# First gated product of a two-block transformer kernel: ten of its eleven column pairs computed as seven block products, with the sums of the fifth modulation row moved ahead of it

## The chip, the core and the metric

One NeuronCore of one Trainium2 chip runs the whole program in one launch. The metric is the device time of that launch in microseconds, and the figure for a kernel is the median of its runs.

## What is computed

Two transformer blocks run one after the other on 512 tokens of width 1024, all in float32. The part that the change rewrites is the gated product of the first block's feed-forward layer, with 2816 hidden features:

```python
h2 = _rmsnorm(x, norm2_w) * (1.0 + scale2) + shift2
ffn = jnp.dot(jax.nn.silu(jnp.dot(h2, w_ffn_gate)) * jnp.dot(h2, w_ffn_up), w_ffn_down)
x = x + gate2 * ffn
```

`gate2` is one of six rows of a modulation `jnp.dot(silu(c), w_ada) + b_ada`; the kernel calls the rows groups 0 to 5, and `gate2` is group 5.

## The kernel before

**Three-pass products.** Each float32 operand is split in a high part (a ScalarE copy to fp32r, L1369 for weights) and a low part (a VectorE subtraction, L1893 for weights), and each product of two operands is three TensorE matmuls: high by high, high by low, low by high (`mm3`). Activations stand split in `Hh`/`Hl` (8 blocks of 128 features by 512 tokens); weights are split, one chunk of 128 x 1024 at a time, into slots of `wh`/`wl` (4 slots) and, in the stages that allow it, two more in `Ah`/`Al`.

**Chunks and ticks.** `weight_plan()` lists all chunks in the order of their loading; `schedule()` walks over the ticks (a tick is the TensorE work that one visit to one chunk gives) and says at each tick which chunks ScalarE splits (`hi_at`), which VectorE finishes or sums (`done`), and which load is issued (`load_at`). Each engine runs its own program in that order and in strict order: an instruction that waits holds back all behind it on its engine. `w.after(n, f)` puts a piece of work n ticks later in an engine's order. Loads are issued by SyncE into four raw buffers in turn; a load into a buffer waits until the chunk in it before has been split or summed.

**The stages around the change**, in order of time: `rp0`, `rp1` (retention projection), `wo0`, `wo1` (output projection; 16 ticks each, each tick six matmuls of 512 columns), `up` and `dn`. In `rp0` to `wo0` VectorE also sums one modulation row (group 4) from eight `ada4` chunks of `w_ada`, each one `scalar_tensor_tensor` into `ACC` (L1890) that needs only its chunk's landing. In `wo0` it also makes the last of the weight sums of the first down product (the four operations on `CST`). `wo0` and `wo1` end each token tile with a residual, two operations `AR<-bank,G` and `X<-X,AR`.

**The up stage.** Pair 0 (gate and up columns 0 to 255) is computed in two halves of 256 tokens, since the second norm is still finishing: eight ticks of 24 matmuls of 256 columns. Pairs 1 to 10 take four ticks each, one for each chunk of two feature blocks, gate and up columns side by side: 24 matmuls of 512 columns. Then ScalarE takes `silu` of two gate banks (L1672), VectorE multiplies by two up banks (`AR<-AR,bank`), and a subtraction of 256 columns prepares the down product. The eight `ada5` chunks lie among the chunks of pairs 2 and 3, and `row_sum` folds their sum on TensorE ahead of pair 6.

**The down stage** `dn` already works with seven block products, 12 matmuls of 512 columns in a full tick, and takes some of its weights from DRAM sums (`sums_dram`) that were made earlier. The sums for the second block's down product are made by GpSimd-issued DMAs that copy (L2815) and add in DRAM (`second_terms` L2820, `third_terms` L2825, `fourth_term` L2829).

## Time and profile before

| | |
|---|---|
| median of 3 runs | 1527.66 us (1526.28 to 1527.98) |
| profiled execution | 1526.64 us, span 1524.8 us |
| TensorE (PE) | busy 1500.3 us, 98% |
| VectorE (DVE) | busy 999.1 us, 66% |
| ScalarE (ACT) | busy 660.8 us, 43% |
| granted clock of PE | 1.00 of full in the up stage |

Times in rows are microseconds from the start of the span. A matmul's own duration includes its passage through the array, so the pace of a stream is read from the distance of starts. Idle time is given ahead of an instruction, with what ended it; of several releasers the one named can have been done long before, and the true one is then mostly a transfer.

### The profile page before, as it was taken

To read this page: it belongs to the slowest core of one execution; us is meant where nothing else is said; L and a number is where in the kernel's file an instruction comes from. 1 tells how busy PE (TensorE), PEld (TensorE's weight loads), DVE (VectorE), ACT (ScalarE), POOL (GpSimd) and SP (SyncE) were. 2 spreads that over 40 slices of the span, in tenths; PEclk is the share of its full clock that TensorE was granted. 3 is DMA by queue.
4 is the path that set the end of the run, shared out by engine and by line. 5 is a ranking of instruction groups with operands and counts; after the bars stand their busy time and mean duration, and the time that the engine had idled before them with its cause. 6 is when DMAs were issued, how large, how long until landed. Compare 5 with 4: busy or idle time off the path is not lost.

```text
span 1524.8 us, 21037 instructions
## 1 busy us (share of the span) xinstructions
PE 1500.3 (98%) x8527; PEld 1224.8 (80%) x8527; DVE 999.1 (66%) x1729; ACT 660.8 (43%) x1090; POOL 64.4 (4%) x93
## 2 busy tenths in 40 slices
PE   7999999999999999999999989999999999999999
PEld 5777887778888898888887767877788988888887
DVE  6679886776588654323358876787567456556885
ACT  4453334653322442222336553766525434434653
POOL 1000000000000011001000021200011000000000
PEclk9999999999999999999999999999999999999999
DMA  9422122159778498967977516100113222232473
GB/s 386 145 82 97 56 70 83 57 187 352 267 273 308 138 350 287 264 163 185 215 172 216 186 60 221 56 30 29 57 56 125 97 101 87 89 110 97 134 230 126
DMA packets 87018, 237.98 MB, mean 156 GB/s; under 512 B 12037, under 2 KB 12165, under 8 KB 85769
## 3 DMA queue, kind: packets, MB, share of 16 engines
q1 hardware_dynamic: 68312, 204.87, 38.6%
q0 software_dynamic: 18608, 31.77, 9.5%
q8 instruction: 67, 1.10, 0.3%
q14 instruction: 31, 0.25, 0.1%
HBM read 222.94 MB, written 45.35 MB: 176 GB/s over the span
## 4 chain that ended last, share of the span: by engine, by line
PE 90%; DVE 6%; ACT 3%; issue 1%; POOL 0%; DMA 0%; SPq 0%; DVEq 0%; ACTq 0%
PE bank L689 86%; PE bank L701 4%; DVE AR L1915 1%; DVE wl L1893 1%; DVE Hl L1915 0%; ACT wh L1369 0%; DVE G L1922 0%; DVE AR L2225 0%; DVE X L1915 0%; DVE Al L1893 0%; DVE AR L1918 0%; DVE X L1922 0%; ACT AR L1380 0%; DVE ST L1915 0%; DMA CST<-in_cst 0%
## 5 line engine op out<-in xcount | busy, mean ns | idle before, releaser
L1369 ACT ACTIVATE wh<-raw 128x1024 fp32r<-128x1024 f32 (+1 forms) x223 | 230.7, 1036 | 367.7 <-PE bank L689 290.0
L1893 DVE TENSOR_TENSOR wl<-raw,wh 128x1024 fp32r<-128x1024 f32 (+1 forms) x223 | 263.8, 1193 | 102.0 <-ACT wh L1369 101.9
L689 PE MATMUL bank<-wh,Hh 128*128 128x512 f32 (+1 forms) x726 | 293.1, 404 | 3.8 <-DVE wl L1893 2.5
L689 PE MATMUL bank<-wh,Hl 128*128 128x512 f32 (+1 forms) x726 | 281.1, 387 | 0.0
L689 PE MATMUL bank<-wl,Hh 128*128 128x512 f32 (+1 forms) x726 | 280.4, 386 | 0.0
L689 PE MATMUL bank<-Hh,wh 128*128 128x512 f32 (+2 forms) x712 | 268.5, 377 | 0.5 <-DVE Hl L1915 0.4
L689 PE MATMUL bank<-Hl,wh 128*128 128x512 f32 (+2 forms) x712 | 266.9, 375 | 0.0
L689 PE MATMUL bank<-Hh,wl 128*128 128x512 f32 (+2 forms) x712 | 266.9, 375 | 0.0
L689 PEld LDWEIGHTS bank<-wh,Hh 128*128 128x128 f32 x726 | 136.5, 188 | 38.5 <-issue 9.7
L689 PEld LDWEIGHTS bank<-wh,Hl 128*128 128x128 f32 x726 | 136.3, 188 | 28.4
L689 PEld LDWEIGHTS bank<-wl,Hh 128*128 128x128 f32 x726 | 136.8, 188 | 23.6
L689 PEld LDWEIGHTS bank<-Hh,wh 128*128 128x128 f32 (+1 forms) x712 | 133.7, 188 | 25.4 <-issue 0.7
L689 PEld LDWEIGHTS bank<-Hl,wh 128*128 128x128 f32 (+1 forms) x712 | 133.7, 188 | 24.7 <-issue 0.5
L689 PEld LDWEIGHTS bank<-Hh,wl 128*128 128x128 f32 (+1 forms) x712 | 133.7, 188 | 24.6
L1369 ACT ACTIVATE Ah<-raw 128x1024 fp32r<-128x1024 f32 (+1 forms) x58 | 58.3, 1006 | 122.6 <-PE bank L689 89.8
L1922 DVE SCALAR_TENSOR_TENSOR AR<-bank,PRMT,AR 128x511 f32<-128x511 f32 x88 | 63.8, 746 | 51.0 <-ACT AR L1866 49.5
L689 PE MATMUL bank<-Hh,Ah 128*128 128x512 f32 (+1 forms) x256 | 96.3, 376 | 0.0
L689 PE MATMUL bank<-Hl,Ah 128*128 128x512 f32 (+1 forms) x256 | 96.2, 376 | 0.0
L689 PE MATMUL bank<-Hh,Al 128*128 128x512 f32 (+1 forms) x256 | 96.2, 376 | 0.0
L1893 DVE TENSOR_TENSOR Al<-raw,Ah 128x1024 fp32r<-128x1024 f32 (+1 forms) x58 | 65.9, 1156 | 36.6 <-ACT Ah L1369 36.6
L701 PE MATMUL bank<-CST,AR 128*128 128x128 f32 x513 | 79.7, 282 | 10.2 <-DVE AR L1918 9.2
L1915 DVE TENSOR_TENSOR Hl<-AR,Hh 128x512 fp32r<-128x512 f32 (+2 forms) x62 | 55.2, 904 | 47.3 <-ACT Hh L1657 37.2
(275 smaller groups left out, 2014.3 us busy)
## 6 DMA issues: line engine op xcount, KB each, us to landing
raw<-in_wst SPq DMA_DIRECT2D x224, 512.0 KB, 4.5
sums_dram<-in_down POOLq DMA_DIRECT2D x11, 2816.0 KB, 38.0
raw<-sums_dram SPq DMA_DIRECT2D x40, 512.0 KB, 4.1
raw<-in_down SPq DMA_DIRECT2D x30, 512.0 KB, 4.6
CST<-in_down SPq DMA_DIRECT2D x11, 1024.0 KB, 5.9
sums_dram<-CST SPq DMA_DIRECT2D x11, 1024.0 KB, 4.8
AR<-in_wst SPq DMA_DIRECT2D x8, 1024.0 KB, 11.2
X<-in_x SPq DMA_DIRECT2D x8, 512.0 KB, 5.9
```

Of the source, the lines that this page charges most:

```text
L689: return e.matmul(o, l, r, start=start, stop=stop, skip_group_check=True)
L701: return e.transpose(o, a, C("ident")[0:n, 0:n])
L1369: e.activation(HI[slot[i]][:, 0:width(i)], raw[:, i % NR, 0:width(i)], ACT.Copy).then_inc(*w_hi.mark(i))
L1893: e.tensor_tensor(LO[slot[i]][:, 0:n], raw[:, i % NR, 0:n], HI[slot[i]][:, 0:n].bitcast(f32), SUB).then_inc(*w_lo.mark(i))
L1915: return e.tensor_tensor(o, a, b, op).then_inc(*dve.mark(*events))
L1922: return e.scalar_tensor_tensor(out=o, in0=a, scalar=s, in1=b, op0=op0, op1=op1).then_inc(*dve.mark(*events))
```

## The change

Pairs 1 to 10 of the first up product become seven block products (Winograd's form of Strassen's scheme) over two halves of the 1024 features, two halves of the 512 tokens, and gate against up columns. Each product is 512 features by 256 weight columns by 256 tokens: 24 matmuls of 256 columns, one tick. So a pair has seven ticks, where it had four. Four weight blocks are loaded as before (B11, B12, B21, B22; B12 is used in sums alone), and VectorE forms four sums of them in the raw buffers (`up_sum`: T1 = B11+B12, T3 = B12+B22, T2 = B22+T1, T4 = B21+T2); B11, B21, B22 and T1 to T4 are split. Four sums of the activations are formed once (`up_left_sum`) and split into `Ah`/`Al`, `EH`/`EL` and the right halves of `Hh`/`Hl`. `Ah`/`Al` are thus no slots in this stage. Results are combined by three ScalarE copies out of the banks (`snapshot`), two `silu` and five VectorE operations for each pair, beside the subtraction for `dn`.

The raw buffers get fixed homes (`raw_homes`), with two more in `CST` and a third one for one chunk. The `ada5` chunks move ahead: one behind each of the last two chunks of `rp1` (the other chunks there have `ada4`), and so on through `wo0` and `wo1`, and the last, `ada5.7`, behind the last `ada5` of `wo1`'s chunks. `row_sum` of group 5 moves to the seventh tick of pair 0. The third and fourth terms of the DRAM sums move behind the roots of a later stage on GpSimd's queue. The second norm gets four full buffers instead of two.

```diff
@@ -87,14 +87,16 @@
     among = ada((4,), 1)
     for n in (0, 1):
         block(f"rp{n}", "w_ret_proj", 8, [(512 * n, 512)], among=among, start=1 - n)
+    among += ada((5,), 1)
     for n in (0, 1):
         block(f"wo{n}", "w_out", 8, [(512 * n, 512)], among=among)
-    among = ada((5,), 1)
-    for j in range(11):
-        for c in range(4):
-            plan.append((f"up{j}", c, ("w_ffn_gate", "w_ffn_up"), 2 * c, 2, [(256 * j, 256), (256 * j, 256)]))
-            if j > 1 and among:
-                plan.append(among.pop(0))
+    plan += among
+    for c in range(4):
+        plan.append(("up0", c, ("w_ffn_gate", "w_ffn_up"), 2 * c, 2, [(0, 256), (0, 256)]))
+    for j, z in up_splits():
+        at = {"B11": ("w_ffn_gate", 0), "B21": ("w_ffn_gate", 4), "B12": ("w_ffn_up", 0), "B22": ("w_ffn_up", 4)}
+        w, k = at.get(z, (None, 0))
...
@@ -116,6 +118,65 @@
 
 
+def up_steps():
+
+
+    begin = "B11 1,B21 1,B11 2,B21 2,T1 1,T2 1,B22 1,T3 1,T1 2,T4 1,B22 2,T2 2,B11 3,T3 2,T1 3,T4 2,B22 3,T2 3,B21 3,T3 3"
+    steps = [(int(j), z) for z, j in (x.split() for x in begin.split(","))]
+    for j in range(4, 10):
+        steps += [(j, "B11"), (j, "T1"), (j - 1, "T4"), (j, "B22"), (j, "T2"), (j, "B21"), (j, "T3")]
+    return steps + [(10, "T1"), (10, "B11"), (10, "B22"), (10, "T2"), (9, "T4"), (10, "T3"), (10, "B21"), (10, "T4")]
+
+
+def up_splits():
...
+             (2, "B21"): [(2, "T1")], (1, "T4"): [(2, "T3")], (2, "B22"): [(2, "T2")], (2, "T2"): [(2, "T4")],
+             (3, "B11"): [(3, "T1")], (2, "T4"): [(3, "T3")], (3, "B22"): [(3, "T2")], (3, "T2"): [(3, "T4")]}
+    for j in range(4, 11):
+        after.update({(j, "B11"): [(j, "T1")], (j, "T1"): [(j, "T3")], (j, "B22"): [(j, "T2")], (j, "T2" if j < 10 else "B21"): [(j, "T4")]})
+    return after
+
+
+def raw_homes(chunks, place):
+
+
+    home, queue = {}, {}
+    ring, first = place["2ck", 0], place["up0", 0]
...
@@ -257,6 +318,9 @@
 
     def up(prefix):
         ticks.extend((prefix, (0, a, c), place[f"{prefix}0", c], a > 0) for a in (0, 256) for c in range(4))
+        if prefix == "up":
+            ticks.extend((prefix, (j, z), place["up" + z, j], True) for j, z in up_steps())
+            return
         ticks.extend((prefix, (j, 0, c), place[f"{prefix}{j}", c], True) for j in range(1, 11) for c in range(4))
 
     def seven(key):
...
-        if k and name == "up" and ticks[k - 1][0] == "wo1":
-            avail += [(v, place["wo1", 1]) for v in (NH, NH + 1)]
+        if k and name == "dn" and ticks[k - 1][0] == "up":
...
             avail += [(v, place["2wn1", 1]) for v in (NH, NH + 1)]
         here = max(n for n, p in enumerate(plain) if p <= i)
         done[k] += lows
-        used |= set(lows)
+        for x in lows:
+            use(x)
         lows = []
-        while at < ring and at - NR in used:
+        issue(k)
+        while at < ring and (at in loaded or at in made):
+            mine = chunks[at][0][2:3] in ("B", "T") and chunks[at][0][:2] == "up"
...
@@ -592,8 +696,41 @@
         PART = {"1": 0, "5": 0, "7": 1, "6": 1, "2": 2, "3": 2, "4": 3}
         BLOCK = {"dn": "up", "2dn": "2up"}
         SPLIT_AT = {**{2 * n - 7: n for n in range(4, 15)}, 25: 15, 27: 16, 29: 17, 31: 19, 32: 18, 33: 20}
+        SPLITS = {"dn": {0: 2, 2: 3, **SPLIT_AT}, "2dn": SPLIT_AT}
         LEFT_IN = [*range(5)] * 3 + [1, 2, 3, 5, 0, 6]
         SUMS_AT = {2: ("6", 0), 4: ("6", 1), 6: ("6", 2), 8: ("5", 0), 9: ("5", 1), 10: ("5", 2), 12: ("3", 0), 14: ("3", 1), 16: ("3", 2)}
+
+        ACT2 = A(0, 11264).rearrange("p (j m s) -> p j m s", j=11, m=2)
+        PARTS = A(6144, 4096).rearrange("p (t h q) -> p h t q", t=4, h=2)
+        LU, RG = A(11776, 512), A(12288, 512)
...
@@ -1047,9 +1186,13 @@
             by_tile("wo1", ["wo1"], 8, merged, HM, lambda t, n: dve.of(("wo1", t)), lambda t: w.after(TURN[t], lambda: norm_turn("n2", t)))
 
             def up(prefix, tag, freed, fourth=None):
-                for j, a, c in w.steps(prefix):
...
                         if last and c == 3:
                             free[b] = freed(j, m)
+
+            def up_product(j, z):
+                i, b = place["up" + z, j], up_product_bank(j, z)
+                h, l = split_weights(i)
+                xh, xl = UPLEFT[z]
+                first = z in ("B11", "T1", "B21")
+                on.wait_ge(*w_lo.of(i))
+                if z in UPSUM:
+                    on.wait_ge(*dve.of(("up", "left", z)))
+                if first:
+                    claim(b)
+                elif z == "T2":
+                    on.wait_ge(*act.of(("up", "p1", j)))
+                elif z == "T3":
+                    on.wait_ge(*act.of(("up", "u", j)))
+                elif z == "T4":
+                    on.wait_ge(*dve.of(("up", "c22", j)))
+                else:
+                    on.wait_ge(*act.of(("up", "q5", j)))
+                for m in (0, 1):
+                    for q in range(4):
+                        x = mm3(bank[b][:, 256 * m:256 * m + 256], (h[:, q, tok(m)], l[:, q, tok(m)]), (xh[:, q, :], xl[:, q, :]), first and m + q == 0, q == 3)
+                x.then_inc(*dense.mark(("up", z, j), ("used", i)))
+                if z == "T4":
+                    free[b] = act.of(("up", "right gate", j))
+                elif z == "B22":
+                    free[b] = dve.of(("up", "c12", j))
...
@@ -1656,20 +1828,59 @@
                 on.wait_ge(*(freed or left_free(key, n)))
                 e.activation(hi[:, 0:256 * x.shape[1]].rearrange("p (a q) -> p a q", q=256), x, ACT.Copy).then_inc(*act.mark((key, "left", n)))
 
-            for j, a, c in w.steps("up"):
-                if (j, a, c) == (0, 256, 0):
+            def up_left(z, free):
+                on.wait_ge(*dve.of(("up", "sum", z)))
+                on.wait_ge(*free)
+                for u in (0, 1):
+                    e.activation(UPLEFT[z][0][:, :, tok(u)], up_place(z)[:, u, :].rearrange("p (k q) -> p k q", k=4), ACT.Copy).then_inc(*act.mark(("up", "left", z, u)))
+
+            def snapshot(j, z):
+                e.activation(to, bank[up_product_bank(j, z)][:, :], ACT.Copy).then_inc(*act.mark(("up", event, j)))
+
+            def left_silu(j):
+                on.wait_ge(*dve.of(("up", "c11", j)))
+                e.activation(left_gate(j), left_gate(j), ACT.Silu).then_inc(*act.mark(("up", "left gate", j)))
...
-                e.tensor_tensor(LO[slot[i]][:, 0:n], raw[:, i % NR, 0:n], HI[slot[i]][:, 0:n].bitcast(f32), SUB).then_inc(*w_lo.mark(i))
+                e.tensor_tensor(LO[slot[i]][:, 0:n], raw_of(i), HI[slot[i]][:, 0:n].bitcast(f32), SUB).then_inc(*w_lo.mark(i))
+                for t in formed.get(i, ()):
+                    up_sum(t)
+
+            def up_sum(t):
+
+                z, j = chunks[t][0][2:], chunks[t][1]
+                a, b = {"T1": ("B11", "B12"), "T3": ("B12", "B22"), "T2": ("B22", "T1"), "T4": ("B21", "T2")}[z]
+                for q in (a, b):
+                    if q[0] == "B":
+                        on.wait_ge(*landed(place["up" + q, j]))
+                own()
+                tt(raw_of(t), raw_of(place["up" + a, j]), raw_of(place["up" + b, j]), ADD, ("formed", t))
 
             def right_sums(key, p):
                 b11, b12, b21, b22 = (SUMT[:, 512 * q:512 * q + 512] for q in range(4))
```

**VectorE at the end of `wo0` and the start of `wo1`.** Before, from the split of chunk `wo1.1` to the first residual of `wo1` (`bank3` is the residual of `wo0`'s last tile; the `x2` row is the splits of `wo1.2` and `wo1.3`):

```order
L1893 TENSOR_TENSOR wl<-raw,wh 128x1024 [waits s_w_hi]
L1915 TENSOR_TENSOR CST<-CST 128x512 [waits s_pair]
L1915 TENSOR_TENSOR CST<-CST 128x512 [waits s_dve]
L1915 TENSOR_TENSOR CST<-CST 128x512
L1915 TENSOR_TENSOR CST<-CST 128x512 [waits s_dve]
L1915 TENSOR_TENSOR AR<-bank3,G 128x512 [waits s_dense]
L1915 TENSOR_TENSOR X<-X,AR 128x512 [waits s_x3,s_dve]
L1893 TENSOR_TENSOR wl<-raw,wh 128x1024 [waits s_w_hi] x2
L1915 TENSOR_TENSOR AR<-bank0,G 128x512 [waits s_dense]
```

Of the changed kernel, the same stretch:

```order
L2104 TENSOR_TENSOR wl<-raw,wh 128x1024 [waits s_w_hi]
L2138 TENSOR_TENSOR CST<-CST 128x512 [waits s_pair]
L2138 TENSOR_TENSOR CST<-CST 128x512 [waits s_dve]
L2138 TENSOR_TENSOR CST<-CST 128x512
L2138 TENSOR_TENSOR CST<-CST 128x512 [waits s_dve]
L2101 SCALAR_TENSOR_TENSOR ACC<-raw,ST,ACC 128x1024 [waits s_dve,s_raw1]
L2138 TENSOR_TENSOR AR<-bank3,G 128x512 [waits s_dense]
L2138 TENSOR_TENSOR X<-X,AR 128x512 [waits s_x3,s_dve]
L2104 TENSOR_TENSOR wl<-raw,wh 128x1024 [waits s_w_hi]
L2101 SCALAR_TENSOR_TENSOR ACC<-raw,ST,ACC 128x1024 [waits s_dve,s_raw3]
L2101 SCALAR_TENSOR_TENSOR ACC<-raw,ST,ACC 128x1024 [waits s_dve,s_raw0]
L2104 TENSOR_TENSOR wl<-raw,wh 128x1024 [waits s_w_hi]
```

Three sums of `ada5` chunks (5, 6 and 7) now stand here. The last two stand between the split of `wo1.2` and the split of `wo1.3`; `ada5.7` is loaded into buffer 0 (`s_raw0`), which is that of `wo1.2`, and its load waits for the split of `wo1.2`.

**VectorE as the up stage begins.** Of the changed kernel, from the last low part of the second norm to the first half of pair 0's products (before, two weight splits, two products and a subtraction stood here):

```order
L2138 TENSOR_TENSOR Hl<-AR,Hh 128x4x128 [waits s_act] x2
L2138 TENSOR_TENSOR AR<-AR 128x2x512 [waits s_dve] x4
L2138 TENSOR_TENSOR Al<-AR,Ah 128x4x128 [waits s_act] x4
L2104 TENSOR_TENSOR wl<-raw,wh 128x1024 [waits s_w_hi]
L2151 COPY G<-bank6 128x512 [waits s_dve,s_small]
L2151 COPY G<-bank7 128x512
L2104 TENSOR_TENSOR wl<-raw,wh 128x1024 [waits s_w_hi]
L2138 TENSOR_TENSOR raw<-raw 128x1024 [waits s_dve,s_raw3,s_raw1]
L2138 TENSOR_TENSOR AR<-AR,bank2 128x512 [waits s_dense,s_act]
L2138 TENSOR_TENSOR AR<-AR 128x256 [waits s_dve]
L2138 TENSOR_TENSOR AR<-AR,bank3 128x512 [waits s_dense,s_act]
L2104 TENSOR_TENSOR wl<-AR,wh 128x1024 [waits s_w_hi]
```

The `x4` rows are the four sums of the activations and the low parts of two of them; `bank6` and `bank7` are group 5's row.

**VectorE in a pair of the up stage.** Before, for pair 3 (the multiplications with the up banks, and splits):

```order
L1893 TENSOR_TENSOR wl<-raw,wh 128x1024 [waits s_w_hi] x2
L1915 TENSOR_TENSOR AR<-AR,bank2 128x512 [waits s_dense,s_act]
L1915 TENSOR_TENSOR AR<-AR 128x256 [waits s_dve]
L1915 TENSOR_TENSOR AR<-AR,bank3 128x512 [waits s_dense,s_act]
L1893 TENSOR_TENSOR wl<-raw,wh 128x1024 [waits s_w_hi] x2
L1893 TENSOR_TENSOR Al<-raw,Ah 128x1024 [waits s_w_hi] x2
```

Of the changed kernel, most of one pair's round (`CST` and `raw` are raw buffers; rows without `wl` that write them are the weight sums):

```order
L2138 TENSOR_TENSOR raw<-raw,CST 128x1024 [waits s_dve,s_raw4,s_raw1]
L2104 TENSOR_TENSOR wl<-raw,wh 128x1024 [waits s_w_hi]
L2138 TENSOR_TENSOR AR<-bank2,AR 128x512 [waits s_act,s_dense]
L2138 TENSOR_TENSOR AR<-AR,bank3 128x512 [waits s_dense]
L2104 TENSOR_TENSOR wl<-raw,wh 128x1024 [waits s_w_hi]
L2138 TENSOR_TENSOR CST<-CST,raw 128x1024 [waits s_dve,s_raw2]
L2138 TENSOR_TENSOR AR<-AR,bank1 128x512 [waits s_dense]
L2104 TENSOR_TENSOR wl<-raw,wh 128x1024 [waits s_w_hi]
L2138 TENSOR_TENSOR raw<-raw 128x1024 [waits s_dve]
L2138 TENSOR_TENSOR AR<-AR 128x2x256 [waits s_dve,s_act]
L2104 TENSOR_TENSOR wl<-CST,wh 128x1024 [waits s_w_hi]
L2104 TENSOR_TENSOR wl<-raw,wh 128x1024 [waits s_w_hi]
```

A round has seven splits, four weight sums, and the five operations that combine the banks, where it had four splits and two multiplications.

## Rows read from the trace of the kernel before

**Rows 1.** Page, the span and section 1 (busy us, share, instructions)

```profile
span 1524.8 us, 21037 instructions
...
PE 1500.3 (98%) x8527; PEld 1224.8 (80%) x8527; DVE 999.1 (66%) x1729; ACT 660.8 (43%) x1090; POOL 64.4 (4%) x93
```

**Rows 2.** Pairs 1 to 10: us, busy PE, PEld, DVE, ACT, POOL, clock, DMA share, GB/s

```profile
556.40:776.00 219.60, 219.60 (x966) 180.89 (x965) 80.55 (x85) 58.38 (x66) 12.08 (x7) 1.00 0.86 229
```

**Rows 3.** Waits of PE from 500 to 820: total, times, longest

```profile
PE bank L689 <- DVE Al L1893: 2.5, 1, 2.5
PE bank L689 <- DVE Hl L1915: 0.4, 1, 0.4
```

**Rows 4.** Timeline of ACT in `dn`: start, us, instruction, [idle before <-releaser]

```profile
808.86 1.06 ACT L1369 ACTIVATE Ah<-raw 128x1024 fp32r<-128x1024 f32 x1 [2.78 <-PE bank L689]
```

**Rows 5.** DMA issues from 775 to 860: KB each, median us to landing

```profile
raw<-in_down SPq DMA_DIRECT2D x11, 512.0 KB, 8.3
sums_dram<-in_down POOLq DMA_DIRECT2D x1, 2816.0 KB, 34.8
```

**Rows 6.** Timeline of PE in pair 0, one tick and the next

```profile
541.22 0.28 PE L689 MATMUL bank<-Hh,wl 128*128 128x256 f32 x1
...
544.10 0.28 PE L689 MATMUL bank<-Hh,wl 128*128 128x256 f32 x1
544.82 0.36 PE L689 MATMUL bank<-Hh,wh 128*128 128x256 f32 x1 [0.44 <-DVE Hl L1915]
```

**Rows 7.** Timeline of PE, last tick of pair 5 and row sum

```profile
659.80 0.39 PE L689 MATMUL bank<-Hh,Ah 128*128 128x512 f32 x1
...
665.24 2.14 PE L689 MATMUL bank<-ACC,CST 128*128 128x512 f32 x4
```

**Rows 8.** Timeline of DVE before and in the up stage

```profile
538.41 2.35 DVE L1893 TENSOR_TENSOR Al<-raw,Ah 128x1024 fp32r<-128x1024 f32 x2
...
641.03 0.69 DVE L1915 TENSOR_TENSOR AR<-AR,bank 128x512 f32<-128x512 f32 x1 [5.85 <-PE bank L689]
641.75 0.42 DVE L1915 TENSOR_TENSOR AR<-AR 128x256 f32<-128x256 f32 x1
...
644.35 2.35 DVE L1893 TENSOR_TENSOR wl<-raw,wh 128x1024 fp32r<-128x1024 f32 x2
```

**Rows 9.** Timeline of DVE, end of `wo0` and start of `wo1`

```profile
506.01 1.22 DVE L1893 TENSOR_TENSOR wl<-raw,wh 128x1024 fp32r<-128x1024 f32 x1
507.15 2.74 DVE L1915 TENSOR_TENSOR CST<-CST 128x512 f32<-128x512 f32 x4
509.81 0.68 DVE L1915 TENSOR_TENSOR AR<-bank,G 128x512 f32<-128x512 f32 x1
510.53 0.69 DVE L1915 TENSOR_TENSOR X<-X,AR 128x512 f32<-128x512 f32 x1
511.13 2.35 DVE L1893 TENSOR_TENSOR wl<-raw,wh 128x1024 fp32r<-128x1024 f32 x2
```

**Rows 10.** Timeline of PE in `wo1`: first matmuls of `wo1.2` and `wo1.3`

```profile
512.64 0.39 PE L689 MATMUL bank<-wh,Hh 128*128 128x512 f32 x1
...
514.00 0.39 PE L689 MATMUL bank<-wh,Hh 128*128 128x512 f32 x1
```

**Rows 11.** One line (SyncE's weight loads), issued from 509 to 530

```profile
DMA to landing us min/median/max: 3.2/3.7/4.5
```

**Rows 12.** Timeline of DVE in `rp0`: the sum of one `ada4` chunk

```profile
449.88 1.29 DVE L1890 SCALAR_TENSOR_TENSOR ACC<-raw,ST,ACC 128x1024 f32<-128x1024 f32 x1 [2.17 <-DMA raw<-in_wst]
```

**Rows 13.** Timeline of ACT as pair 0 ends

```profile
554.87 1.28 ACT L1672 ACT_TABLE_LOAD   x1
556.16 1.09 ACT L1672 ACTIVATE AR<-bank 128x512 f32<-128x512 f32 x2
```

**Rows 14.** SyncE's weight loads issued from 540 to 780

```profile
DMA to landing us min/median/max: 5.5/7.8/13.5
```

**Rows 15.** Timeline of POOL, a later norm's next root

```profile
956.04 0.24 POOL L2834 TENSOR_SCALAR ST<-ST 128x8 f32<-128x8 f32 x1 [10.49 <-DVE ST L1925]
```

More of the change, by code:

```diff
@@ L338, in schedule @@
             avail.append((slot[i], i))
-        while load < ring and load - NR in used:
-            load_at[k].append(load)
-            load += 1
+        issue(k)
     assert at == ring
-    return place, ticks, hi_at, done, load_at, slot, before
+    return place, ticks, hi_at, done, load_at, slot, before, home, queue, formed
 def program(nc, x_in, cst_in, prm_in, bc_in, brow_in, wst, down_in, out):
@@ L352, in program @@
     chunks = weight_plan()
[L353 removed]
+    place, ticks, hi_at, done_at, load_at, slot, before, home, queue, formed = schedule(chunks)
     pair_load_at, pair_sum_at, pair_store_at = summing(ticks)
```

274 lines of the change are left out of this document (221 added, 53 removed).

## The prediction

> **What bounds the kernel now.** I read the page first: PE is busy 98% of the span and DVE 66% [rows 1], so time is saved only where PE gets less to do or waits less. Then the stretch that the change rewrites, pairs 1 to 10: PE is busy for all of its 219.6 us, DVE for 80.6, ACT for 58.4, the granted clock is 1.00 and the DMA engines carry 229 GB/s [rows 2]. It is bound by PE with nothing in front of it. PE's waits from 500 to 820 show what the neighbours leave to gain: 0.44 us where the up stage begins and 2.5 us in `dn` [rows 3]. Nothing else waits there, in `wo1` neither.
>
> The 2.5 us in `dn` is put down to a split by DVE, but ahead of that split ACT idled 2.78 us, by the record for a bank that had long been done [rows 4]. So it was a landing. The loads of that stretch take 8.3 us, while the fourth DRAM sum, 2816 KB, is under way for 34.8 us [rows 5].
>
> **The products.** A tick of 24 matmuls of 256 columns takes 2.88 us (541.22 to 544.10, 0.120 each) [rows 6]; one of 512 columns takes 5.44 us (659.80 to 665.24, 0.2267 each) [rows 7]. Forty ticks of the second kind, 217.6 us, become seventy of the first, 201.6: **-16.0**. The row sum's 2.1 us [rows 7] only moves. The granted clock is the full 2.4 GHz throughout [rows 2]. The Trainium skill, page "TensorE: Matmul & The Clock Gate", section "Back-to-back issue gap", gives N/2.4 + 2.5 ns for one warm matmul after another: 109 ns for 256 columns and 216 for 512. By it the seventy ticks would be 183 us. Neither row agrees (120 and 226.7), and the sum goes by the rows.
>
> **Start of the up stage.** Two splits into `Al` (2.35 us, [rows 8]) no longer stand on DVE ahead of the norm's last low part, for which PE waits 0.44 us [rows 6]: **-0.5**, and the second half of pair 0 begins at about 544.2 on the clock of before.
>
> **`dn`.** The third and fourth DRAM sums are moved to a later stage, so nothing large runs beside `dn`'s loads: **-2.5**. If the loads stay as late, nothing is gained. On GpSimd's queue these DMAs now stand between a norm's roots, where that queue idles 10.5 us ahead of one of them [rows 15]; only their issue costs there, a few us, so nothing.
>
> **`wo1`.** Here a wait is added. Before, DVE finishes the split of `wo1.1` at 507.15, the sums on `CST` by 509.8, the residual by 511.1, and splits `wo1.2` and `wo1.3` from 511.13 on [rows 9]; PE wants them at 512.64 and 514.00 [rows 10]. Now an `ada5` sum stands ahead of the residual. I take 1.2 us each by the 1.29 of such a sum [rows 12] less the overlap with the next. So `wo1.2` is split by 513.5 instead of 512.3: PE waits 0.9. Then comes the sum of `ada5.6` (514.7) and that of `ada5.7`. Its buffer is the one of `wo1.2`, so its load is issued at 513.5, after that split, and lands 3.7 us later (3.2 to 4.5, [rows 11]), at 517.2. Its sum ends at 518.4, and only behind it comes the split of `wo1.3`, done at 519.6. PE wanted it at 514.00; the first wait (0.9) is part of this delay, so the two together are 519.65 less 514.0: **+5.7** (5 to 7 by the landings). There is a precedent: in `rp0` DVE waited 2.17 us for a chunk of `ada4` to land [rows 12]. `ada5.0` to `ada5.4` cost DVE 1.2 us each among splits that are early: nothing, or 1.3 if one of them waits.
>
> **The first seven-product pairs.** DVE has more ahead of it than PE. From 542.3, when it is done with the norm (544.8 less 2.35): four activation sums (4.8 us at 1.2 per 1024 columns, by the splits of [rows 8]), four half low parts (2.4), the split of B11 (1.15), the wait for the row sum and two copies of it (2.4), a split and the first weight sum (2.3), the wait for `silu` with its table load of 1.28 us [rows 13] (2.1 in all), two multiplications and a difference (0.69, 0.42, 0.69, [rows 8], 1.75 together), three times a split with a sum (7.1), the low parts of two left operands (2.5), a gate operation (0.7) and the split of T1.1 (1.15). That ends at 570.7. PE is there at 544.2 + 8 x 2.88 + 1.9 = 569.1: a wait of **1.7**.
>
> Four ticks later, at 582.3, PE wants T1 of pair 2, whose bank is freed by DVE's subtraction for pair 1. Ahead of that subtraction on DVE stand the weight sum T3.2, a split and the sum T2.2. T3.2 needs B22 of pair 2, whose load can be issued only at about 573.4, when the sum T4.1 has read its buffer's neighbours. Landings in this stage take 5.5 to 13.5 us, 7.8 in the middle [rows 14]. With 7.8 the subtraction ends at 573.4 + 7.8 + 1.2 + 1.15 + 1.2 + 0.7 = 585.4: a wait of **3.1**; with 5.5 0.8, with 13.5 8.8. Both waits: **+4.8** (2.5 to 10.5).
>
> **The steady pairs.** Per pair DVE does seven splits (7 x 1.14), four weight sums (4 x 1.2), five operations of 512 columns (5 x 0.69) and the difference (0.42): 16.7 us, against PE's 7 x 2.88 = 20.2. ACT does seven splits of 1.06 [rows 4] and five operations of 1.09 [rows 13], 12.9. So PE stays the bound on average. The order is tight at two places. The T1 split stands 3.3 us ahead of PE. The T3 product must find ACT's snapshot of the T2 product done, which has 1.2 us. The load of B11 has time up to a landing of about 10.8 us. The median is 7.8 with 229 GB/s moved; now the same weights move in 16 us less, but the large DRAM copies thin out. I allow a late landing here and there: **+1.0** (0 to 5).
>
> **Sum.** -16.0 - 0.5 - 2.5 + 5.7 + 4.8 + 1.0 = -7.5. The profiled execution took 1526.64, so 1519.1; the median of the runs is 1.0 above that execution: **1520**.
>
> **The rivals.**
> *Small stalls.* The waits are the lower ends: 5.0 in `wo1`, 2.5 at the start, 0 in the steady pairs. -16 - 0.5 - 2.5 + 7.5 = -11.5: 1516, down to 1511 if the wait in `wo1` is half, because `ada5.7` lands into a buffer earlier than I read it. For it: landings of 3.2 exist. Against it: DVE's order is fixed, and both waits rest on durations seen in rows. Chance 0.2.
> *A wait in every pair* (the other sign). The load of B11 for the next pair but one is issued when the split of the present one frees its buffer; beyond 10.8 us of landing ACT's split is late, and behind it in ACT's queue stand the snapshot and the `silu` that free PE's banks. At 13.5 us, the longest of [rows 14], it costs 2.7 us per pair: +27, about 1546. It ends slower than before from 0.75 us per pair, a landing of 11.6. For it: the maximum is beyond that, and a burst of loads follows each freed buffer. Against it: the median is 3 us short of it and loads only add where they are late each time. Chance 0.2, and half of that above 1530.
> *DVE as the bound.* DVE would have to take 21 us per pair instead of 16.7, from waits inside its chain (sum, split by ACT, low part) that no row of before has. Three of the seven splits are of sums that DVE made just before. At 1 us over PE in each of ten pairs: 1529. Chance 0.08.
> *The pace of 256-column matmuls.* If it were exactly half of the 512 pace, 0.1133, the stage would save 27 instead of 16: 1509. Twenty-four of them in the kernel itself at 0.120 say no, and PEld's busy share gives no sign of loads being the limit at 512. By the skill's gap of 109 ns, cited above, it would be 18 less than my sum, about 1502. Chance of either 0.02.
>
> **How the numbers follow.** The forecast case, all terms as above within their ends, spans 1515.5 to 1524: chance 0.5. Small stalls, 1510 to 1515.5: 0.2. The per-pair wait and the DVE bound, 1524 to 1546: 0.28. Pace: 0.02. A median of this kernel can be told from another by about 0.2%, 3.1 us, so "same" is 1524.6 to 1530.7. Faster takes the first, second and last case, 0.72, and a little of the third; of the rest 0.12 lies within and 0.15 above. The range 1512 to 1530 leaves out some 0.05 below and 0.15 above.
>
> **What the profile after would show.** PE's waits: one or two for DVE's low part `wl` in `wo1`, together near 5.7 us, with DVE idle before an `ACC` sum with a landing as its end, and none for `Al` in `dn`. A tick of pairs 1 to 10 at 2.88 us. PE waiting for DVE at the first T1 product and once more four ticks on, by about 1.7 and 3.1. DVE busy some 17 us per 20.2 in the steady pairs and PE without gaps there. The prediction is wrong if PE waits once or twice in every pair, if the pace of 256 columns differs in these products, or if `ada5.7` is there in time.

## The result and the profile after

The changed kernel takes 1535.17 us in the median of five runs (1531.15 to 1536.48), the kernel before 1527.34 (five runs). The ratio is 1.0047, with a 95% interval of 1.0033 to 1.0061: half a per cent slower, where 1520 and "faster" were forecast. The profiled execution has a span of 1534.7 us and took 1536.48.

The page, span and section 1, of the changed kernel (compare [rows 1]):

```profile
span 1534.7 us, 22724 instructions
...
PE 1493.5 (97%) x9247; PEld 1252.1 (82%) x9247; DVE 1107.4 (72%) x1841; ACT 710.6 (46%) x1158; POOL 63.9 (4%) x93
```

PE is busy for 6.8 us less than before and yet the span is 9.9 us longer. So the time went into waits, and "busy" hides a second part: PE is also busy when its clock is halved. The same places of the program in the two timelines of PE say where (the first matmul of `wo0`, the first transposition of the second norm, the first matmul of `dn`, the first transposition of the norm behind `dn`):

| place | before | after | later by |
|---|---|---|---|
| `wo0` begins | 483.59 | 487.13 | 3.5 |
| the second norm's first turn | 520.80 | 539.35 | 18.6 |
| `dn` begins | 776.06 | 785.70 | 9.6 |
| the next norm's first turn | 883.57 | 890.04 | 6.5 |
| end of the span | 1524.8 | 1534.7 | 9.9 |

2.5 us are lost before `rp1`. From there to the middle of `wo1` 16.1 us are lost, the up stage gives 8.9 back, `dn` 3.2, and 3.4 are lost behind it. The waits of PE from 440 to 620 (columns as in [rows 3]; before there was one of 0.44 us):

```profile
PE bank L828 <- DVE wl L2104: 9.3, 4, 5.7
PE bank L828 <- DVE Hl L2138: 3.1, 2, 1.7
PE bank L828 <- DVE AR L2138: 2.9, 1, 2.9
```

The stretches of 4 us in which PE ran slow, and the last one in between at full clock (columns as in [rows 2]):

```profile
500.00:504.00 4.00, 4.00 (x11) 3.14 (x10) 3.86 (x8) 0.00 (x0) 0.00 (x0) 0.52 0.45 170
504.00:508.00 4.00, 4.00 (x19) 3.25 (x19) 2.10 (x4) 0.00 (x0) 0.00 (x0) 1.00 0.66 219
...
528.00:532.00 4.00, 1.43 (x3) 1.16 (x4) 2.42 (x2) 0.00 (x0) 0.00 (x0) 0.50 0.39 132
532.00:536.00 4.00, 4.00 (x14) 3.16 (x13) 1.39 (x2) 0.96 (x1) 0.00 (x0) 0.68 0.38 143
...
604.00:608.00 4.00, 4.00 (x19) 4.00 (x20) 3.23 (x4) 0.00 (x0) 1.22 (x2) 0.50 0.08 26
```

Read the PE column together with the clock: from 500 to 504 PE is busy for all 4 us and starts 11 matmuls, from 504 to 508 it starts 19. The granted clock is at half, 1.2 instead of 2.4 GHz. Each such stretch begins within a wait of PE or just behind one.

**`wo1`.** VectorE, from the split of `wo1.2` to that of `wo1.3`:

```profile
521.88 1.22 DVE L2104 TENSOR_TENSOR wl<-raw,wh 128x1024 fp32r<-128x1024 f32 x1
523.02 1.28 DVE L2101 SCALAR_TENSOR_TENSOR ACC<-raw,ST,ACC 128x1024 f32<-128x1024 f32 x1
528.09 1.28 DVE L2101 SCALAR_TENSOR_TENSOR ACC<-raw,ST,ACC 128x1024 f32<-128x1024 f32 x1 [3.80 <-DMA raw<-in_wst]
529.29 1.22 DVE L2104 TENSOR_TENSOR wl<-raw,wh 128x1024 fp32r<-128x1024 f32 x1
```

and PE, which waits for both splits:

```profile
523.15 0.50 PE L828 MATMUL bank<-wh,Hh 128*128 128x512 f32 x1 [1.00 <-DVE wl L2104]
...
530.57 0.79 PE L828 MATMUL bank<-wh,Hh 128*128 128x512 f32 x1 [5.74 <-DVE wl L2104]
```

This is the chain of the prediction: the sum of `ada5.7` waits 3.80 us for its landing while the split of `wo1.3` stands behind it. The load is issued at 523.1 and takes 4.9 us, where the prediction had 3.7.

**`wo0`.** Three waits that the prediction did not have: 1.08 us at 472 in `rp1`, and 1.38 and 1.72 us here, where ACT is late with the high part of `wo0.3` and its next piece of the left operand is late behind it:

```profile
496.31 1.06 ACT L1541 ACTIVATE wh<-raw 128x1024 fp32r<-128x1024 f32 x1 [4.30 <-DMA raw<-in_wst]
```

```profile
495.79 0.47 PE L828 MATMUL bank<-wh,Hh 128*128 128x512 f32 x1 [1.38 <-DVE Hl L2138]
499.38 0.77 PE L828 MATMUL bank<-wh,Hh 128*128 128x512 f32 x1 [1.72 <-DVE Hl L2138]
```

The wait at 472 has its origin 15 us earlier. VectorE stands before the four sums on `CST` until a load of `CST` has landed, and from there to the split for which PE waits it is never idle for more than 0.1 us. After and before:

```profile
457.05 2.75 DVE L2138 TENSOR_TENSOR CST<-CST 128x512 f32<-128x512 f32 x4 [1.38 <-DMA CST<-in_down]
...
470.74 1.22 DVE L2104 TENSOR_TENSOR wl<-raw,wh 128x1024 fp32r<-128x1024 f32 x1
```

```profile
453.07 2.74 DVE L1915 TENSOR_TENSOR CST<-CST 128x512 f32<-128x512 f32 x4
```

(The section on the change lets the `ada5` chunks begin behind chunks of `rp1`. In the plan `ada5.0` stands behind `wo0.1`, and so on to `ada5.6` behind `wo1.3`, with `ada5.7` after it. A load is issued some time before PE comes to its place in the plan: the first, that of `ada5.0`, at 470.2, while PE works on `rp1`.)

**The up stage.** PE at the first T1 product and four ticks later, and then the window from 620 to 770:

```profile
589.14 0.39 PE L828 MATMUL bank<-Ah,wh 128*128 128x256 f32 x1 [1.46 <-DVE wl L2104]
603.81 0.55 PE L828 MATMUL bank<-Ah,wh 128*128 128x256 f32 x1 [2.89 <-DVE AR L2138]
```

```profile
620.00:770.00 150.00, 150.00 (x1252) 150.00 (x1251) 123.50 (x128) 74.05 (x89) 1.90 (x1) 1.00 0.70 177
```

Behind 604 there is no wait until 777. DVE is busy 123.5 of 150 us, 16.6 us for each pair of 20.16.

**Behind `dn`.** PE at the first products of a later norm, after, and the same row of before:

```profile
909.67 1.69 PE L840 MATMUL bank<-CST,AR 128*128 128x128 f32 x8 [3.00 <-DVE AR L2141]
```

```profile
901.07 1.09 PE L701 MATMUL bank<-CST,AR 128*128 128x128 f32 x8 [0.89 <-DVE AR L1918]
```

DVE, which has the operand to make, has a weight split in front of it that waits 2.17 us for ACT:

```profile
905.60 1.23 DVE L2104 TENSOR_TENSOR wl<-raw,wh 128x1024 fp32r<-128x1024 f32 x1 [2.17 <-ACT wh L1541]
```

### The profile page after: what moved, and what is told of

Read it like the earlier page. It is cut to its first block, busy times and chain, and to the rows that moved or that the text cites. A ratio compares the mean times of both kernels' runs of the same rounds, so it can differ in the third digit from the quotient of the medians.

```text
span 1534.7 us, 22724 instructions
## 1 busy us (share of the span) xinstructions
PE 1493.5 (97%) x9247; PEld 1252.1 (82%) x9247; DVE 1107.4 (72%) x1841; ACT 710.6 (46%) x1158; POOL 63.9 (4%) x93
## 4 chain that ended last, share of the span: by engine, by line
PE 79%; DVE 11%; DMA 4%; ACT 4%; issue 2%; POOL 0%; SPq 0%; DVEq 0%; ACTq 0%
PE bank L828 75%; PE bank L840 4%; DVE wl L2104 3%; DVE AR L2138 2%; DMA raw<-in_wst 2%; DVE Hl L2138 1%; ACT wh L1541 1%; DMA raw<-sums_dram 1%; DVE CST L2138 1%; DVE X L2138 1%; DMA raw<-in_down 1%; DMA CST<-in_down 1%; DVE ACC L2101 0%; DMA X<-in_x 0%; DVE G L2145 0%
## 5 line engine op out<-in xcount | busy, mean ns | idle before, releaser
L1541 ACT ACTIVATE wh<-raw 128x1024 fp32r<-128x1024 f32 (+1 forms) x250 | 261.3, 1047 | 354.7 <-PE bank L828 266.8
L2104 DVE TENSOR_TENSOR wl<-raw,wh 128x1024 fp32r<-128x1024 f32 (+1 forms) x250 | 300.1, 1208 | 96.6 <-ACT wh L1541 96.6
L828 PE MATMUL bank<-wh,Hh 128*128 128x512 f32 (+1 forms) x732 | 298.2, 407 | 13.8 <-DVE wl L2104 9.5
L828 PE MATMUL bank<-Hh,wh 128*128 128x256 f32 (+2 forms) x824 | 278.4, 338 | 1.6 <-DVE wl L2104 1.1
L828 PE MATMUL bank<-Hl,wh 128*128 128x256 f32 (+2 forms) x824 | 276.7, 336 | 0.0
L828 PE MATMUL bank<-Hh,wl 128*128 128x256 f32 (+2 forms) x824 | 276.6, 336 | 0.0
L828 PEld LDWEIGHTS bank<-Hh,wh 128*128 128x128 f32 (+1 forms) x824 | 156.3, 190 | 19.1 <-DVE wl L2104 1.5
L828 PEld LDWEIGHTS bank<-Hh,wl 128*128 128x128 f32 (+1 forms) x824 | 156.2, 190 | 16.6
L840 PEld LDWEIGHTS bank<-CST,AR 128*128 128x128 f32 x513 | 62.5, 144 | 32.2 <-issue 13.4
L2138 DVE TENSOR_TENSOR AR<-AR 128x512 f32<-128x512 f32 (+3 forms) x98 | 68.1, 696 | 8.0 <-ACT AR L1978 3.8
L828 PE MATMUL bank<-Ah,wh 128*128 128x256 f32 (+1 forms) x192 | 59.4, 309 | 4.4 <-DVE AR L2138 2.9
```

Source lines behind the costliest of these rows:

```text
L828: return e.matmul(o, l, r, start=start, stop=stop, skip_group_check=True)
L840: return e.transpose(o, a, C("ident")[0:n, 0:n])
L1541: e.activation(HI[slot[i]][:, 0:width(i)], raw_of(i), ACT.Copy).then_inc(*w_hi.mark(i))
L2104: e.tensor_tensor(LO[slot[i]][:, 0:n], raw_of(i), HI[slot[i]][:, 0:n].bitcast(f32), SUB).then_inc(*w_lo.mark(i))
L2138: return e.tensor_tensor(o, a, b, op).then_inc(*dve.mark(*events))
```

## The experiments

What a lower clock cost is taken from starts: in a stretch, the distance between the starts of PE's matmuls, less 0.2267 us for each of 512 columns and 0.120 for each of 256, less the waits. By this sum the changed kernel loses 5.9 us from 460 to 545, 2.8 from 590 to 620; the kernel before 1.3 and 0.0. All ratios are to the kernel before, run beside; where a kernel is set against the changed one, the two ratios are compared. By the intervals, a difference of two ratios is then known to some 2.5 us either way (an estimate), while a kernel against the kernel before is known to 1.5 to 2.

| kernel | median us | ratio (95%) |
|---|---|---|
| changed | 1535.2 | 1.0047 (1.0033 to 1.0061) |
| two_sums_later | 1527.9 | 1.0015 (1.0005 to 1.0025) |
| early_free | 1530.4 | 1.0015 (1.0005 to 1.0026) |
| old_dram | 1541.2 | 1.0099 (1.0084 to 1.0114) |
| sums_alone | 1537.7 | 1.0074 (1.0059 to 1.0089) |
| late_sums | 1528.6 | 1.0015 (1.0006 to 1.0025) |
| late_2kv | 1530.2 | 1.0024 (1.0014 to 1.0033) |
| combined | 1521.0 | 0.9957 (0.9944 to 0.9970) |
| dram_alone | 1522.8 | 0.9975 (0.9964 to 0.9985) |
| small_loads | 1519.1 | 0.9955 (0.9941 to 0.9969) |
| small_sums | 1517.3 | 0.9940 (0.9928 to 0.9953) |
| spread | 1518.8 | 0.9952 (0.9940 to 0.9964) |
| quiet | 1522.8 | 0.9981 (0.9972 to 0.9990) |

### The part with the sums of group 5, undone and alone

(The buffers of the first up chunks are counted from the end of `up0` to fit, here and in spread.)

```diff
+    among.insert(0, plan.pop())
-    plan += among
     for c in range(4):
         plan.append(("up0", c, ("w_ffn_gate", "w_ffn_up"), 2 * c, 2, [(0, 256), (0, 256)]))
+        if among:
+            plan.append(among.pop(0))
```

> The changed kernel with the chunks ada5.6 and ada5.7 loaded, and summed on VectorE, behind up0.0 and up0.1, so after the split of wo1.3 (nothing is left out). My theory: the wait of 5.74 us at wo1.3 came from the sum of ada5.7 standing ahead of that split and from its late load, and the 2.6 us that PE then ran at the half clock came from that wait. Both go, and most of the 1.0 us wait before it: about 9 us below the changed kernel, 1526. Rival A, the clock falls there for another reason than the wait: only 6.7 us, the rows at 0.5 clock stay near that place. Rival B, the wait only moves to the split of up0.0 or up0.1: no gain, a PE wait of 3 to 6 us at the end of wo1 or at the start of the up stage. The waits of wo0 (1.08, 1.38, 1.72) stay in each case.

The gain on the changed kernel is 0.32% of 1527, 4.9 us, about half of what was expected. The wait of 5.74 us is gone, and so is the half clock behind it. But in its profile the wait at 472 was 1.98 us instead of 1.08, with a half-clock stretch behind it (3.6 us from 460 to 545), and three small waits of 0.61, 0.78 and 0.41 us stand at 542 to 546, where the two sums now share DVE with the second norm. Rival B in part: some of the wait moved.

```diff
     for n in (0, 1):
         block(f"rp{n}", ...)
+    among += ada((5,), 1)
     for n in (0, 1):
         block(f"wo{n}", ...)
-    among = ada((5,), 1)
+    plan += among
```

> The kernel before with only one part of the change: the ada5 chunks placed as in the changed kernel, its row sum and the up stage as before (nothing left out). My theory: the waits of wo0 (1.08, 1.38, 1.72 us), of wo1 (1.0, 5.7) and the 5.3 us at the half clock behind them all belong to this part: 14 to 17 us slower than before, 1542 to 1544, less up to 1 us that pairs 2 and 3 gain. Rival: the three waits in wo0 belong to another part (raw buffers, norm buffers), then only the 5.7 and its clock show: +8 to +9, 1536.

0.74%, 11.3 us slower. Its PE timeline shows the wait of `wo0` in one piece, and that of `wo1`:

```profile
494.95 0.76 PE L688 MATMUL bank<-wh,Hh 128*128 128x512 f32 x1 [3.19 <-DVE Hl L1914]
...
527.53 0.79 PE L688 MATMUL bank<-wh,Hh 128*128 128x512 f32 x1 [6.43 <-DVE wl L1892]
```

Together with 0.47 and 0.99 us these are 11.1 us of waits, and the clock cost 5.1 instead of 1.3. The sum, 15 us, was expected. It is 11.3 because the 2.5 us wait in `dn` and its clock loss (4 us) are gone here as well. The fourth DRAM sum is issued at 775.6, as before the change (775.4), but `dn` begins at 791.9 instead of 776.1; the sum ends at 806.7, some 23 us ahead of the place where PE waited before. So the waits in `wo0` belong to this part of the change, without any seven-product pair.

### The DRAM sums

```diff
             copies()
             second_terms()
+            third_terms()
+            fourth_term()
```

> The changed kernel with the third and fourth DRAM sums issued right behind the second ones, as before the change (one part undone, nothing left out). My theory: the fourth sum then runs beside dn's first loads again, a PE wait of some 2.5 us with a stretch at half clock behind it comes back in dn, +3 to +5 us: 1538 to 1540. Rival: the wait of before came from the order of dn's splits, which the change also altered (the first left operands split two ticks apart), so nothing comes back: within 1 us of the changed kernel.

0.52% above the changed kernel, 8 us; more than the 3 to 5 expected, and the rival is out. PE in `dn`:

```profile
806.17 0.50 PE L828 MATMUL bank<-wh,Hh 128*128 128x512 f32 x1 [3.20 <-DVE wl L2104]
812.50 0.50 PE L828 MATMUL bank<-Ah,EH 128*128 128x512 f32 x1 [0.33 <-DVE Al L2104]
823.85 0.50 PE L828 MATMUL bank<-wh,Hh 128*128 128x512 f32 x1 [1.18 <-DVE wl L2104]
```

4.7 us of waits, and 2.9 more at the lower clock from 780 to 835 (3.3 against 0.4): 7.6 us in all. The two profiled spans differ by 3.3 us only (1538.0 and 1534.7), since this execution lost some 5 us less than that of the changed kernel at the half clock in `wo0`, `wo1` and the up stage. The clock's part of a size differs from one execution to the next, and the match of 7.6 with the 8 of the medians is in part luck.

```diff
             second_terms()
-            third_terms()
-            fourth_term()
...
             for name in ("ks", "kw"):
                 root(ST[:, 48:56], dve.of((name, "sum")), (name, "root"))
+            third_terms()
...
+            fourth_term()
             for t in range(T):
                 root(ST[:, 48:52], dve.of(("lsum", t)), ("lroot", t))
```

> The kernel before with only the third and fourth DRAM sums moved as the change moves them (nothing is left out). My theory: the 2.5 us wait in dn and the 1.9 us at the lower clock behind it go: 4 us below before, ratio 0.997. Rival: the crowd around dn's loads is made by the second sums and the eight ada5 chunks of pairs 2 and 3, the wait stays: ratio 1.000.

The ratio is 0.9975, 3.8 us faster, and no wait of PE is left in `dn` before 876; from 780 to 835 the clock costs nothing, where before it cost 1.9. This part of the change pays by itself.

### The start of the up stage

```diff
-                        w.after(3, lambda j=j: left_ups(j))
+                        w.after(1 if j == 1 else 3, lambda j=j: left_ups(j))
```

> The changed kernel with VectorE's subtraction that frees bank 2 of pair 1 placed two ticks earlier, ahead of the weight sum T3.2 that waits for a landing (nothing is left out). My theory: the 2.89 us wait at the second T1 product goes, and the 2.8 us at the half clock behind it: 5 to 6 us below the changed kernel, near 1529.5. Rival A: the half clock at 604 is not caused by the wait, gain 2.9. Rival B: something else is late at the same place (T4.1's low part, which now stands behind the subtraction, or T2.2's), the wait moves by a tick: gain under 1.

0.32%, 4.9 us, near the 5 to 6 expected; the medians alone would not tell it from Rival A's 2.9. The wait is 0.71 us, and the 2.8 us of slow clock behind it have become 0.2.

```profile
603.52 0.36 PE L828 MATMUL bank<-Hh,wh 128*128 128x256 f32 x1 [0.71 <-DVE AR L2138]
```

### A rule for the sums, a chunk of `2kv`, and all three

```diff
             if at in sums:
+                if chunks[at][0] == "ada5" and (lows or loaded[at] + 2 > k):
+                    break
                 done[k].append(at)
```

> The changed kernel with one rule added to its schedule: the sum of an ada5 chunk never stands between the high and the low part of a weight split on VectorE, and not before two ticks after its load (nothing is left out; the ring of buffers stays as it is). My theory: the sums themselves and their landings, in front of splits and of the low parts of the merged rows, made the waits of wo0 (1.38, 1.72 us) and wo1 (1.0, 5.74) and the 5.3 us at the half clock behind them: about 14 us below the changed kernel, 1521 (ratio to the kernel before 0.996). Rival A: the waits of wo0 come from the eight extra loads, which crowd those of wo0.2 and wo0.3, and stay: 1525. Rival B: sums later mean loads of the up stage later, the wait moves there: 1530 and more.

4.9 us, where 14 were expected. In `wo1` the rule does what it is for; in `wo0` it does not:

```profile
498.08 0.47 PE L830 MATMUL bank<-wh,Hh 128*128 128x512 f32 x1 [3.18 <-DVE Hl L2140]
521.15 0.50 PE L830 MATMUL bank<-wh,Hh 128*128 128x512 f32 x1 [0.81 <-DVE wl L2106]
523.48 0.50 PE L830 MATMUL bank<-wh,Hh 128*128 128x512 f32 x1 [0.68 <-DVE wl L2106]
```

6.7 us of waits in `wo1` became 1.5, and a wait of 1.55 us is new at 532. The 3.1 us of `wo0` stay, in one piece: the size of Rival A, whose cause is taken up below.

```diff
-                if name == "dn" and chunks[at][0] == "2kv" and chunks[at][1] > 1 + (what[0] > 45):
+                if name == "dn" and chunks[at][0] == "2kv" and chunks[at][1] > 1 + (what[0] > 46):
```

> The changed kernel with the high part of chunk 2kv.2 held back by one tick at the end of dn, where the kernel before has it (nothing is left out). My theory: VectorE then no longer splits the next chunk ahead of the products for the last norm, and the wait of 3.0 us at 909 falls to the 0.9 us of before: 2 to 3 us below the changed kernel, 1532.5. Rival: the place on VectorE is set by other chunks (2kw) and nothing moves: within 0.5 us, below what this comparison tells.

0.23%, 3.5 us below the changed kernel by the ratios. The wait of 3.00 us is back at the 0.89 of before. The intervals are 2 us wide each way, so the size agrees with 2 to 3 as well as with 3.5.

The three edits of late_sums, early_free and late_2kv in one kernel:

> The changed kernel with the three edits together: the rule for the ada5 sums, the early subtraction that frees bank 2 of pair 1, and 2kv.2 one tick later (nothing is left out). My theory: the gains add, 14 + 5 + 2.5 us, 1514 (ratio 0.991). Rival: the half clock comes at other waits instead, and the gain is that of the waits alone, about 13 us: 1522.

Ratio 0.9957, 6.6 us faster than before and 13.8 below the changed kernel. The gains of the three single edits, 4.9, 4.9 and 3.5, add to 13.3. The 14 that had been set down for the first of them were wrong, not the adding.

### What makes `wo0` wait

The four kernels of this section are combined with one more edit each. The first two leave out a part of the data of group 5's sum, so their results are wrong and only their times count.

```diff
+                if key == "ada5":
+                    e.dma_start(raw_of(i)[:, 0:64], stream(i)[:, 0:64]).then_inc(s_raw[home[i]], 16)
+                    return
                 e.dma_start(part_of_raw(i), stream(i)).then_inc(s_raw[home[i]], 16)
```

> The kernel of the three edits (combined), with the loads of the eight ada5 chunks cut to their first 64 of 1024 columns; so the sum of group 5 is formed of wrong data, and only its time counts. Crowding theory: the wait of 3.2 us at the second tick of wo0 is ACT's split of wo0.3, which waits for a landing among eight extra loads (6.6 us in the middle there, where before 6.0 to 6.4), so it goes to under 1 us and so does the half clock behind it (2 to 3 us); with the 0.8, 0.7 and 1.6 us in wo1 mostly staying, 5 us below combined, 1516. Rival, VectorE's time: the sums themselves stand ahead of the low parts for which PE waits; then the wait stays at 2 us or more.

The wait at the second tick of `wo0` is 2.32 us, not under 1, and the kernel is no faster than combined by these intervals (0.9955). So the data of the `ada5` loads is not the main part of what makes the chunk late.

```profile
498.67 0.47 PE L830 MATMUL bank<-wh,Hh 128*128 128x512 f32 x1 [2.32 <-DVE Hl L2140]
```

```diff
-                    acc = ACC[:, g % 2, :]
-                    e.scalar_tensor_tensor(out=acc, in0=raw_of(i), ...)
+                    m = 64 if g == 5 else 1024
+                    acc = ACC[:, g % 2, 0:m]
+                    e.scalar_tensor_tensor(out=acc, in0=raw_of(i)[:, 0:m], ...)
```

> The kernel of the three edits (combined), with the sums of the eight ada5 chunks over the first 64 of 1024 columns; so the rest of group 5's row is left without its sum, and only the time counts. The loads are whole. Crowding theory: the wait in wo0 falls only by the 1.2 us of the one sum that stands ahead of the low parts, to 2 us, and the waits of wo1 (0.8, 0.7) go: 3 us below combined, 1518. Rival, VectorE's time: the wait of wo0 goes to under 1 us, with the half clock, 6 us below combined.

Ratio 0.9940, 2.6 us below combined, which is not clear of the noise. In `wo1` no wait of 0.8 and 0.7 is left. That at 472 is gone too, but the first shortened sum comes only behind that place. In `wo0`:

```profile
497.53 0.47 PE L830 MATMUL bank<-wh,Hh 128*128 128x512 f32 x1 [2.16 <-DVE Hl L2141]
```

Neither theory as it was put. Cutting the data takes 0.9 us off the 3.18, cutting the sums 1.0, and 2.2 to 2.3 stay under each. What both kernels kept is the turn in the four raw buffers. Before, the load of `wo0.3` is issued when the split of `wo0.0` is done; in the changed kernel `wo0.2` has that place and `wo0.3` waits for the split of `wo0.1`, two ticks later, since `ada5.0` has a buffer that `wo0.2` had. The traces show it: against the start of `wo0`, the load of `wo0.3` is issued 4.2 us earlier in the kernel before, and 0.1 us later in all ten kernels with `ada5` chunks in `wo0`, these two among them. It lands 7.7 us behind the start of `wo0` in combined and 6.8 in small_loads, and PE waits 3.18 and 2.32, each time what exceeds 4.5. In small_sums it lands at 7.7 and PE waits what exceeds 5.5. A load issued at that moment lands at 7.3 in the kernel before too (that of `wo1.1`, which is needed much later). So the turn alone makes some 1.8 us of the 3.18 (an estimate, 7.3 less 5.5), the largest part; the sums make 1.0 and the later landing the rest.

```diff
-    among += ada((5,), 1)
-    for n in (0, 1):
-        block(f"wo{n}", "w_out", 8, [(512 * n, 512)], among=among)
+    block("wo0", "w_out", 8, [(0, 512)], among=among)
+    among = ada((5,), 1)
+    block("wo1", "w_out", 8, [(512, 512)], among=among)
...
+        plan.append(among.pop(0))
```

> The kernel of the three edits (combined), with the ada5 chunks spread over a longer stretch: one behind each chunk of wo1 and one behind each of up0's, none in wo0 (nothing is left out). Crowding theory: four fewer loads land in rp1 and wo0, the waits at 472 and 499 go to under 1 us each: minus 4 to 6 us; the sums beside the second norm cost up to 2 back: ratio to the kernel before 0.993, 1516. Rival: VectorE is busy as the second norm is made (21.8 of 24 us before) and each sum there is a wait of PE: no gain or a loss of up to 3 us against combined.

In this kernel `wo0.3` is loaded at the split of `wo0.0` again, 4.0 us ahead of `wo0`, and lands at 2.3. The wait at 499 is gone:

```profile
472.68 0.50 PE L830 MATMUL bank<-Hh,wh 128*128 128x512 f32 x1 [1.83 <-DVE wl L2106]
517.83 0.50 PE L830 MATMUL bank<-wh,Hh 128*128 128x512 f32 x1 [0.81 <-DVE wl L2106]
...
541.09 0.39 PE L830 MATMUL bank<-Hh,wh 128*128 128x256 f32 x1 [1.70 <-DVE AR L2140]
```

The edit also takes the `ada5` loads and sums out of `wo0`, so it doesn't part them from the turn. The issue times and the two kernels above do, and they make the turn the largest part of the wait, not all of it. The gain against combined is not clear of the noise (0.9952 against 0.9957), since 2.7 us of waits came in beside the second norm (1.70, 0.41, 0.56): the rival's mechanism took most of it. This kernel, 7.3 us below before, and combined are the fastest of those that compute the whole.

The wait at 472 did not go. It was 1.08 to 1.98 us in ten of the kernels, 0.47 in sums_alone, and absent in small_sums. The `ada5` chunks are not its cause, since their first load is issued at 470.2. In each of the ten it is the idle time of VectorE ahead of the sums on `CST` (1.38 to 2.27 us) less 0.3; in small_sums that idle time is 0.16, as the load of `CST` took 7.1 us there and 8.3 to 9.2 in the ten. In the changed kernel SyncE issues a load of `raw` that waits for a sum of `ada4` ahead of the load of `CST` (448.36 and 448.73); before, it stood behind it (445.51 and 447.74). This order comes with the new rule for the raw buffers. No run takes it back alone, so its share is not shown.

```diff
-    among += ada((5,), 1)
-    for n in (0, 1):
-        block(f"wo{n}", "w_out", 8, [(512 * n, 512)], among=among)
+    block("wo0", "w_out", 8, [(0, 512)], among=among)
+    among = ada((5,), 1)
+    block("wo1", "w_out", 8, [(512, 512)], among=among)
     plan += among
```

> The kernel of the three edits, with no ada5 chunk in wo0, one behind each chunk of wo1 and the last four behind those in the quiet middle of wo1, where VectorE splits no weights (nothing is left out). Occupancy theory: wo0.2 and wo0.3 get their raw buffers as early as before the change, so the wait at 499 is gone as in the spread kernel, and the waits beside the second norm (1.7, 0.4, 0.6 us there) are not there: 2 to 3 us below spread, 1516, ratio to the kernel before 0.9935. Rival: four sums in a row in wo1, two of them behind landings, hold back wo0's or wo1's residual, for which PE waits: the wait is there in place of the others, ratio 0.995 or above.

It is a miss, 0.9981. DVE and then PE in `wo1`:

```profile
521.37 5.45 DVE L2103 SCALAR_TENSOR_TENSOR ACC<-raw,ST,ACC 128x1024 f32<-128x1024 f32 x4 [1.83 <-DMA raw<-in_wst]
526.74 0.69 DVE L2140 TENSOR_TENSOR AR<-bank,G 128x512 f32<-128x512 f32 x1
```

```profile
531.21 1.97 PE L842 MATMUL bank<-CST,AR 128*128 128x128 f32 x8 [5.71 <-DVE AR L2143]
```

Four sums and a landing, 7.3 us in all, stand ahead of the residual of the first token tile. The second norm needs that residual and PE needs the norm: a wait of 5.71 us. The stretch looked quiet only because what DVE has to do in it is short; it is not early.

## Why the prediction was wrong

The forecast was 7.5 us of gain and the measurement is 7.8 us of loss, beyond the range. By its own steps:

- **The products, -16.0: right.** 24 matmuls of 256 columns take 2.88 us from 620 to 770 (1252 records in 150 us, 0.1198 each), at a granted clock of 1.00. With 0.2267 for 512 columns this is (N + 32) / 2.4 ns for N columns at both widths (no other was looked at), so halving the columns doesn't quite halve the time: at half of 0.2267 the seventy ticks would take 190.4 us, and not 201.6.
- **Start of the up stage, -0.5, and `dn`, -2.5: right in place.** No wait of 0.44 at 544 and none of 2.5 in `dn`. old_dram and dram_alone show the DRAM sums as its cause, and in sums_alone, where they stand as before but the fourth is over before PE comes to the place, PE doesn't wait. The size was off by the clock: it is 3.8 us alone.
- **`wo1`, +5.7: right in mechanism, 6.7 in waits** (1.00 and 5.74); the landing of `ada5.7` was 1.2 us longer than its 3.7. Where it failed is in what follows a wait: PE ran at the half clock up to 534, 2.6 us more. The sum has no term for this at any of its waits, and gives no reason.
- **"`ada5.0` to `ada5.4` cost DVE 1.2 us each among splits that are early: nothing, or 1.3": the step that failed.** It counted time on DVE and left out that each extra chunk takes a turn in the four raw buffers. The chunk behind it is loaded one split later: `wo0.3` 4.2 us later against `wo0`. That made 1.38 and 1.72 us of waits, and 2.7 at the half clock with them. sums_alone shows that this part of the change is enough to cause them; the issue times, the two kernels with less data or work, and spread show that the turn is the largest part.
- **Not in the sum at all: 1.08 us in `rp1`.** A load of `CST` landed later and held VectorE, before any `ada5` load was issued. The changed order of SyncE's loads is the likely reason; no run tests it.
- **The first seven-product pairs, +4.8: 4.35 in waits** (1.46 and 2.89), at both places named. early_free shows the second and its 2.8 us of slow clock, which the sum did not have.
- **The steady pairs, +1.0: 0.5.** One wait of 0.47 us. DVE's 16.7 us for each pair was 16.6. Both rivals that would hold back every pair are out: landings in the up stage took 6.7 us in the middle and at most 9.1, short of the 10.8 that would count.
- **Not in the sum at all: 3.4 us behind `dn`.** The changed order of slots lets 2kv.2 be split a tick earlier, DVE gets a waiting split in front of a norm, and PE waits 2.1 us more. late_2kv undoes it.
- **Not the change's work, as far as is seen: 2.5 us before `rp1`, 2.1 of them in the first 20.** The second tile of the input is read by ACT at 8.48, before at 7.20, behind the same DMAs in the same order:

```profile
8.48 1.06 ACT L1552 ACTIVATE AR<-X 128x1024 f32<-128x1024 f32 x1 [2.23 <-DMA X<-in_x]
```

```profile
7.20 1.06 ACT L1380 ACTIVATE AR<-X 128x1024 f32<-128x1024 f32 x1 [0.81 <-DMA X<-in_x]
```

  A part of this delay is in the profile of dram_alone too, which has the old up stage (PE's first stream of 512 columns begins at 19.91 there, 20.04 in the changed kernel, 17.90 before), and quiet, which has the new one, begins at 18.26. So the new up stage is not its cause. Why the landing differs between programs whose first DMAs are alike stays open.

Summed up: 2.5 + 16.1 - 8.9 - 3.2 + 3.4 = 9.9 us of span. The largest gap is the 16.1 where 5.7 stood: 4.2 us of waits in `rp1` and `wo0`, 1.0 more in `wo1`, 4.6 us at the half clock (5.9 less 1.3), and the rest in small distances. Over the whole kernel the slow clock makes up 7 of the 17 us by which the profiled execution missed the forecast (4.6 in `wo0` and `wo1`, 2.8 in the up stage, 1.0 behind `dn`, less 1.5 in `dn`), the largest single part, which the prediction had at nothing; the waits in `rp1` and `wo0` are 4.2, the norm behind `dn` 2.1, the start 2.5.

The slower rival of the prediction was another mechanism (landings in every pair); what happened was in none of the rivals. One of the prediction's sums does not come out: with half of its wait in `wo1`, the rival of small stalls ends near 1513.5 and not at 1511.
